# The trunk's buffers begin at multiples of 2048 bytes, and the score passes alternate between row halves

## The chip, the cores and the metric

The kernel runs on one core of a Trainium2 chip. The core has a tensor engine (TensorE, "PE" in the profile, with its weight loads shown apart as "PEld"), a vector engine (DVE), a scalar engine (ACT), a general engine (POOL) and a queue of transfers issued by SyncE (SP). They run side by side and meet only at semaphores. The metric is the device time of one execution, in microseconds; it is 1284.3 us before the change (median of 3 runs, 1284.09 to 1289.94).

## The reference

One sequence of 512 positions, width 1024, all in float32, goes through two layers:

```python
def reference(x, ...):
    # layer 0: convolution module, then gated FFN
    x = conformer_conv_module(x, ...)      # norm, 1024x2048 matmul, depthwise conv 31 taps, norm, 1024x1024 matmul
    x = conv_ffn(x, ...)                   # norm, 1024x5632 matmul, depthwise conv 3 taps, silu(gate)*up, 2816x1024
    # layer 1: differential attention, then gated FFN
    k_sh = rms_norm((rms_norm(x) @ w_k).reshape(b, s, 8, 2, 64)); v_sh = (rms_norm(x) @ w_v).reshape(b, s, 8, 128)
    q = rms_norm((rms_norm(x) @ w_q).reshape(b, s, 8, 2, 64))
    # 8 heads, 2 components c of 64 channels each, blocks of 128 query rows
    scores = einsum('bqhcd,bkhcd->bhcqk', q, k) * 64 ** -0.5
    probs = softmax(where(causal, scores, -1e30))
    diff = probs[:, :, 0] - lam * probs[:, :, 1]
    x = x + rms_norm(diff @ v) * (1 - lam_init) @ w_o
    x = conv_ffn(x, ...)
```

## The kernel before, in words

Every float32 matmul is made of three passes over rounded parts: each operand is split into a high part and the remainder (`_hi` and `_lo`, type float32r), and the passes are high x high, high x low and low x high. The activations stand channel-major: `x`, `xg_hi`, `xg_lo` (the normed input of a projection) and `act_hi`, `act_lo` (the input of the second matmul of a layer part) are 8 tiles each of 128 channels by 512 positions, 2048 bytes in each partition. A tile is the moving operand of a matmul of 512 columns at line 1034, and a 128 x 128 piece of `w_hi` or `w_lo` (512 bytes in each partition) is its stationary operand.

Weights come as one stream of 99 units of up to 128 x 2048 numbers into `w_raw`, which has two slots. ACT makes `w_hi` of a unit and DVE makes `w_lo`, one unit ahead of PE. With the input projections PE reads `xg_hi` and `xg_lo` (832 times three passes), with the output projections `act_hi` and `act_lo` (480 times three passes). For keys, queries and values the roles are swapped (line 1152): the stationary operand is a piece of `xg`, the moving one is 256 columns of a weight unit, 1024 bytes, so the starts of moving pieces alternate between two places 1024 bytes apart. In the convolution (line 1088) the stationary operand is a diagonal matrix `diag` and the moving one is `u_hi` or `u_lo` from column t on for tap t, so its start moves by 4 bytes with each tap and by 2168 bytes from tile to tile.

The attention's order is written out by hand. `attention_schedule` calls, for each of 96 pieces of the key, query and value projections, `dense` (12 matmuls of line 1152) and then the steps of `SLOTS` for the current head: turning keys and queries by transposes (`turn K`, `turn Q`), three sets of score blocks (`score A`: query block 3; `score B`: blocks 2 and 0; `score C`: block 1), softmax on ACT (line 661) with maxima on DVE (line 970), the difference of the components on DVE (`differ`, lines 979 to 982), its transposes (`turn A`, `B`, `C`, line 1171), and the product with the values (line 1214). All engines go through the same list in the same order. Block b of queries sees (b + 1) x 128 keys, so its score matmul has 512, 384, 256 or 128 columns.

Component c of a head lies in partitions 64c to 64c + 63 of `qT` and `kT`, so a score matmul uses 64 rows of the array. Its result goes to bank 4 for component 0 and to bank 5 for component 1. In `scores` PE takes one component after the other. For each block it runs the three passes and then the causal mask, a matmul of `ident16` and `mask16` in bfloat16 that uses all 128 rows and adds -1e30 above the diagonal; the mask's matmul signals `s_done`. PE waits for `e_done`, the exponentials of the set before, ahead of each set.

All of SBUF is placed by `put`, one buffer behind the other, each rounded up to 64 bytes. The build's first free byte is 16,481, so `top` is 16,512, which is 128 past a multiple of 2048. `x`, `xg_hi`, `xg_lo`, `w_raw`, `w_hi` and `w_lo` have sizes that are multiples of 2048 and all begin at 128 past a multiple of it. Behind them come parameters and constants of other sizes, and `act_hi` begins at 119,616, which is 832 past a multiple. `act_lo`, `kT`, `qT`, `v_hi` and `u_hi` also begin at 832 past a multiple.

Of the kernel before, what the change touches and what calls it, by code (L numbers as in the profile page):

```python
# [31 lines left out]
P = 128  # L32
# [9 lines left out]
HD = 64  # L42
# [59 lines left out]
SETS = [[3], [2, 0], [1]]  # L102
# [3 lines left out]
COLUMN = {3: 0, 2: 0, 0: 3 * P, 1: 0}  # L106
# [64 lines left out]
def trunk(nc, x_t, stream, params, lambdas, out_t):  # L171
    with ExitStack() as ctx:
# [4 lines left out]
            return ctx.enter_context(nc.semaphore(name))  # L177


        top = -(-nc.sbuf_base // 64) * 64  # L180

        def put(name, at, shape, dtype=F32):

            size = 2 if dtype == BF16 else 4
            end = at + -(-math.prod(shape[1:]) * size // 64) * 64
            return nc.alloc_sbuf_tensor_at(name, shape, dtype, offset=at)[(slice(None),) * len(shape)], end


        x, at = put("x", top, [P, KT, SEQ])
        xg_hi, at = put("xg_hi", at, [P, KT, SEQ], F32R)  # L190
        xg_lo, at = put("xg_lo", at, [P, KT, SEQ], F32R)
        w_raw, at = put("w_raw", at, [P, RING, SLOT])
        w_hi, at = put("w_hi", at, [P, RING, SLOT], F32R)
        w_lo, at = put("w_lo", at, [P, RING, SLOT], F32R)
        par, at = put("par", at, [P, N_PARAMS])
        ident, at = put("ident", at, [P, P])
        ones, at = put("ones", at, [P, P])
        ident16, at = put("ident16", at, [P, P], BF16)
        mask16, at = put("mask16", at, [P, P], BF16)
        small, at = put("small", at, [P, 112])  # L200

        conv_area = at
        act_hi, at = put("act_hi", at, [P, KT, SEQ], F32R)
        act_lo, area = put("act_lo", at, [P, KT, SEQ], F32R)
        eps = small[:, 0:1]
# [19 lines left out]
        sq, at = put("sq", area, [P, 2, SEQ])  # L225
        sq_sum, at = put("sq_sum", at, [P, SEQ])
        rs, at = put("rs", at, [P, SEQ])
# [3 lines left out]
        ffn_u, at = put("ffn_u", own_area, [P, 4, UP])  # L231
        ffn_t, at = put("ffn_t", at, [P, 4, SEQ])

        CP = SEQ + TAPS - 1
        conv_u, at = put("conv_u", conv_area, [P, KT, CP])
        diag, at = put("diag", at, [P, DIAGS, len(PE_TILES), 2, P], F32R)
        assert at <= area
        conv_a, at = put("conv_a", own_area, [P, 2, SEQ])
        conv_b, at = put("conv_b", at, [P, SEQ])
        conv_c, at = put("conv_c", at, [P, KT, SEQ])  # L240
        ln_sq, at = put("ln_sq", at, [P, 2, SEQ])
        u_hi, at = put("u_hi", at, [P, len(PE_TILES), CP], F32R)
        u_lo, at = put("u_lo", at, [P, len(PE_TILES), CP], F32R)
        dw_hi, at = put("dw_hi", at, [P, KT * TAPS], F32R)
        dw_lo, at = put("dw_lo", at, [P, KT * TAPS])
        lam_in, at = put("lam_in", at, [P, 4, HD])
        lam_prod, at = put("lam_prod", at, [P, 2, HD])

        v_hi, at = put("v_hi", area, [P, 2, TB, 2 * VD], F32R)
        v_lo, at = put("v_lo", at, [P, 2, TB, 2 * VD], F32R)  # L250
        k_sb, at = put("k_sb", at, [P, 2, TB, 2 * P])
        q_sb, at = put("q_sb", at, [P, 2, TB, 2 * P])
        kq_sq, at = put("kq_sq", at, [P, TB, 2 * P])
        kT_hi, at = put("kT_hi", at, [P, SEQ], F32R)
        kT_lo, at = put("kT_lo", at, [P, SEQ], F32R)
        qT_hi, at = put("qT_hi", at, [P, SEQ], F32R)
        qT_lo, at = put("qT_lo", at, [P, SEQ], F32R)
        dT_hi, at = put("dT_hi", at, [P, 10 * P], F32R)
        dT_lo, at = put("dT_lo", at, [P, 10 * P], F32R)
        prob, at = put("prob", at, [P, 2, 2, SEQ])  # L260
        o_sb, at = put("o_sb", at, [P, TB, VD])

        bank = [ctx.enter_context(nc.psum_tensor(f"bank{n}", [P, SEQ], F32)) for n in range(8)]
# [93 lines left out]
        block = ctx.enter_context(nc.Block())  # L357
# [669 lines left out]
        def _(pe):  # L1027
# [54 lines left out]
            for t in range(TAPS):  # L1082
                for n, m in enumerate(PE_TILES):
# [3 lines left out]
                    for s, (w, u) in enumerate(((0, u_hi), (0, u_lo), (1, u_hi))):  # L1087
                        got = pe.matmul(bank[CONV[n]][:, :], diag[:, t % DIAGS, n, w, :], u[:, n, t:t + SEQ],  # L1088
                                        start=(t == 0 and s == 0), stop=(t == TAPS - 1 and s == 2), skip_group_check=True)
# [84 lines left out]
            def scores(h, n):  # L1174

                if 8 * h + 2 * PLACE[SETS[n][0]]:
                    pe.wait_ge(e_done, 8 * h + 2 * PLACE[SETS[n][0]])
                for c in range(2):
                    for b in SETS[n]:
                        out = bank[4 + c][:, COLUMN[b]:COLUMN[b] + (b + 1) * P]  # L1180
                        rows = slice(c * HD, (c + 1) * HD)
                        qs = slice(b * P, (b + 1) * P)
                        for s, (q, k) in enumerate(((qT_hi, kT_hi), (qT_hi, kT_lo), (qT_lo, kT_hi))):
                            pe.matmul(out, q[rows, qs], k[rows, 0:(b + 1) * P],  # L1184
                                      start=s == 0, stop=False, skip_group_check=True)

                        pe.matmul(out[:, b * P:(b + 1) * P], ident16[:, :], mask16[:, :], start=False, stop=True,  # L1187
                                  skip_group_check=True).then_inc(s_done, 1)

            def step(h, name):  # L1190
# [16 lines left out]
                elif name == "output":  # L1207
                    pe.wait_ge(dT_l, 3 * h + 3)
                    pe.wait_ge(turned_lo, min(2 * h + 3, 2 * HEADS))
                    for b in range(TB):  # L1210
                        for k in range(b + 1):
                            at = TRI[b] + k * P
                            for n, (d, v) in enumerate(((dT_hi, v_hi), (dT_hi, v_lo), (dT_lo, v_hi))):
                                got = pe.matmul(bank[7][:, b * VD:(b + 1) * VD], d[:, at:at + P], v[:, g % 2, k, cols],  # L1214
                                                start=(k == 0 and n == 0), stop=(k == b and n == 2), skip_group_check=True)
                    got.then_inc(o_done, 1)
                elif name == "turn output":
                    pe.wait_ge(o_normed, h + 1)
                    for b in range(TB):
                        got = pe.transpose(bank[7][:, b * P:(b + 1) * P], o_sb[:, b, :], ident[:, :])  # L1220
                    got.then_inc(oT_done, 1)
                elif name == "score A":
                    pe.wait_ge(turned_lo, 2 * h + 2)
                    scores(h, 0)
                elif name.startswith("score"):
                    scores(h, LETTER[name[-1]])
                elif name == "turn A":
                    turn(h, 0)
                elif name == "turn B":
                    pe.wait_ge(dT_l, 3 * h + 1)  # L1230
                    turn(h, 1)
                elif name == "turn C":
                    pe.wait_ge(dT_l, 3 * h + 2)
                    turn(h, 2)
# [75 lines left out]
```

## Time and profile before

| what | value |
|---|---|
| median of 3 runs | 1284.3 us |
| the profiled execution's own time | 1283.49 us |
| its span, first to last instruction | 1281.7 us |
| mean granted TensorE clock | 0.991 of full |
| PE busy | 1238.3 us, 97% of the span |
| PEld busy | 1021.3 us, 80% |
| DVE busy | 843.0 us, 66% |
| ACT busy | 544.3 us, 42% |
| DMA | 81 GB/s over the span |

A busy PE in the profile is not a PE at its peak: the end of a matmul is modelled, and one matmul's shown duration laps over the next. The distance from one start to the next is what a matmul costs in a row of them. Where a stretch runs at the full granted clock, TensorE is at 2.4 GHz; at half it is at 1.2 GHz.

### The profile page before, as it was taken

The numbers are of one execution on the slowest core, as the hardware profiler recorded it, in microseconds if no ns is written. First come the engines' busy times: TensorE is split into PE (matmuls) and PEld (weight loads), VectorE is DVE, ScalarE is ACT, GpSimd is POOL, SyncE is SP. The second block draws the span as 40 slices with busy tenths as digits, with TensorE's granted clock in tenths as the row PEclk, the third lists the DMA queues.
The fourth block names the chain that finished last, engine by engine and source line by source line (L and its number), as shares of the span: only waits on it lengthen the run. The fifth ranks groups of instructions, "written<-read, shape, count | busy, mean of one in ns | idle before, by whom it ended". The sixth has DMA issues, their size and how long they took to land.

```text
span 1281.7 us, 16583 instructions
## 1 busy us (share of the span) xinstructions
PE 1238.3 (97%) x6085; PEld 1021.3 (80%) x6085; DVE 843.0 (66%) x1158; ACT 544.3 (42%) x942; POOL 111.2 (9%) x99
## 2 busy tenths in 40 slices
PE   6998997999999999999999999997999999999999
PEld 4787756788888888887998889966888888888887
DVE  7999946577627763676577777665577537762673
ACT  6256955444314431345454545433444324431441
POOL 4000001200000000002324141401200000000000
PEclk9999998999999999999999999998999999999999
DMA  5221001222322222223221212211222322232222
GB/s 212 81 91 59 1 5 53 98 76 98 109 89 98 98 99 99 81 74 109 96 70 34 67 34 67 66 33 33 99 94 91 111 69 96 98 118 79 99 74 91
DMA packets 16615, 104.00 MB, mean 81 GB/s; under 512 B 1840, under 2 KB 1968, under 8 KB 5424
## 3 DMA queue, kind: packets, MB, share of 16 engines
q1 hardware_dynamic: 16560, 103.25, 24.2%
q8 instruction: 36, 0.59, 0.2%
q14 instruction: 19, 0.16, 0.0%
HBM read 101.15 MB, written 2.10 MB: 81 GB/s over the span
## 4 chain that ended last, share of the span: by engine, by line
PE 89%; DVE 6%; ACT 3%; POOL 1%; issue 1%; DMA 0%; SPq 0%; POOLq 0%; DVEq 0%; ACTq 0%
PE bank L1034 67%; PE bank L1152 9%; PE bank L1088 5%; PE bank L1184 2%; PE bank L1214 2%; POOL sq_sum L415 1%; DVE w_lo L707 1%; DVE w_lo L699 1%; ACT prob L661 1%; DVE prob L980 1%; PE bank L1105 1%; PE bank L1187 1%; DVE prob L982 1%; PE bank L1079 1%; DMA w_raw<-stream 0%
## 5 line engine op out<-in xcount | busy, mean ns | idle before, releaser
L1034 PE MATMUL bank<-xg_hi,w_hi 128*128 128x512 f32 x832 | 326.8, 393 | 13.6 <-DVE xg_lo L715 11.1
L1034 PE MATMUL bank<-xg_lo,w_hi 128*128 128x512 f32 x832 | 325.0, 391 | 0.0
L1034 PE MATMUL bank<-xg_hi,w_lo 128*128 128x512 f32 x832 | 325.0, 391 | 0.0
L470 ACT ACTIVATE w_hi<-w_raw 128x2048 fp32r<-128x2048 f32 x83 | 158.3, 1907 | 156.5 <-PE bank L1034 156.5
L699 DVE TENSOR_TENSOR w_lo<-w_raw,w_hi 128x2048 fp32r<-128x2048 f32 x83 | 192.6, 2320 | 30.9 <-ACT w_hi L470 30.9
L1034 PE MATMUL bank<-act_hi,w_hi 128*128 128x512 f32 x480 | 193.2, 402 | 8.9 <-DVE act_lo L831 7.2
L1034 PEld LDWEIGHTS bank<-xg_hi,w_hi 128*128 128x128 f32 x832 | 156.9, 189 | 48.3 <-DVE w_lo L730 11.1
L1034 PE MATMUL bank<-act_lo,w_hi 128*128 128x512 f32 x480 | 190.8, 398 | 0.0
L1034 PE MATMUL bank<-act_hi,w_lo 128*128 128x512 f32 x480 | 190.6, 397 | 0.0
L604 ACT ACTIVATE ffn_t<-ffn_u,par 128x512 f32<-128x512 f32 x88 | 72.0, 818 | 268.6 <-DVE ffn_u L884 268.6
L1034 PEld LDWEIGHTS bank<-xg_lo,w_hi 128*128 128x128 f32 x832 | 157.0, 189 | 33.3 <-issue 0.7
L1034 PEld LDWEIGHTS bank<-xg_hi,w_lo 128*128 128x128 f32 x832 | 156.9, 189 | 32.8
L1034 PEld LDWEIGHTS bank<-act_hi,w_hi 128*128 128x128 f32 x480 | 91.1, 190 | 33.0 <-issue 8.0
L1152 PE MATMUL bank<-w_hi,xg_hi 128*128 128x256 f32 x384 | 113.7, 296 | 1.0 <-DVE xg_lo L715 1.0
L1152 PE MATMUL bank<-w_lo,xg_hi 128*128 128x256 f32 x384 | 109.1, 284 | 0.0
L1152 PE MATMUL bank<-w_hi,xg_lo 128*128 128x256 f32 x384 | 109.1, 284 | 0.0
L1034 PEld LDWEIGHTS bank<-act_hi,w_lo 128*128 128x128 f32 x480 | 90.9, 189 | 22.4
L1034 PEld LDWEIGHTS bank<-act_lo,w_hi 128*128 128x128 f32 x480 | 91.0, 190 | 21.1
L846 DVE TENSOR_TENSOR x<-bank,x 128x512 f32<-128x512 f32 x56 | 38.5, 688 | 102.2 <-PE bank L1034 102.2
L891 DVE SCALAR_TENSOR_TENSOR ffn_t<-ffn_u,par,ffn_t 128x512 f32<-128x512 f32 x88 | 65.8, 748 | 56.1 <-ACT ffn_t L604 56.1
L884 DVE TENSOR_TENSOR ffn_u<-bank,rs 128x512 f32<-128x512 f32 x88 | 60.5, 688 | 42.3 <-PE bank L1034 42.2
L1152 PEld LDWEIGHTS bank<-w_hi,xg_hi 128*128 128x128 f32 x384 | 74.3, 194 | 1.3 <-DVE xg_lo L715 1.2
(141 smaller groups left out, 1607.6 us busy)
## 6 DMA issues: line engine op xcount, KB each, us to landing
w_raw<-stream SPq DMA_DIRECT2D x87, 1024.0 KB, 4.9
w_raw<-stream SPq DMA_DIRECT2D x8, 768.0 KB, 4.3
x<-x_t SPq DMA_DIRECT2D x8, 256.0 KB, 6.8
out_t<-x SPq DMA_DIRECT2D x8, 256.0 KB, 2.0
w_raw<-stream SPq DMA_DIRECT2D x2, 512.0 KB, 5.1
par<-params SPq DMA_DIRECT2D x1, 345.5 KB, 2.9
lam_in<-lambdas SPq DMA_DIRECT2D x1, 128.0 KB, 8.6
```

Source lines behind the costliest of these rows:

```text
L415: pool.tensor_tensor(sq_sum, sq_sum, sq[:, k % 2, :], ALU.add).then_inc(sq_added, 1)
L470: act.activation(w_hi[:, j, :], w_raw[:, j, :], ACT.Copy).then_inc(w_hi_done, 1)
L604: act.activation(ffn_t[:, 2 * j + s, :], ffn_u[:, 2 * j + s, FTAPS - 1:UP], ACT.Identity, bias=p("ffn_dw_b", at + t), scale=p("ffn_dw_w", ...
L699: dve.tensor_tensor(w_lo[:, j, :], w_raw[:, j, :], w_hi[:, j, :].bitcast(F32), sub).then_inc(w_lo_done, 1)
L846: new = dve.tensor_tensor(x[:, k, :], b, x[:, k, :], ALU.add)
L884: dve.tensor_tensor(u[:, FTAPS - 1:UP], bank[2 * j + s][:, :], rs, ALU.mult).then_inc(u_done, 1)
L891: own.wait(own.mark(dve.scalar_tensor_tensor(out=v, in0=u[:, 1:1 + SEQ], scalar=p("ffn_dw_w", w + 1), in1=v, op0=ALU.mult, op1=ALU.add)))
L1034: got = pe.matmul(out, weights(w, j, k, m), v[:, k, :], start=(k == 0 and s == 0), stop=(k == count - 1 and s == 2), skip_group_check=True)
L1088: got = pe.matmul(bank[CONV[n]][:, :], diag[:, t % DIAGS, n, w, :], u[:, n, t:t + SEQ], start=(t == 0 and s == 0), stop=(t == TAPS - 1 and ...
L1152: got = pe.matmul(out, v[:, k, b * P:(b + 1) * P], w[:, j, k * 2 * P:(k + 1) * 2 * P], start=(k == 0 and s == 0), stop=(k == KT - 1 and s ...
L1184: pe.matmul(out, q[rows, qs], k[rows, 0:(b + 1) * P], start=s == 0, stop=False, skip_group_check=True)
L1214: got = pe.matmul(bank[7][:, b * VD:(b + 1) * VD], d[:, at:at + P], v[:, g % 2, k, cols], start=(k == 0 and n == 0), stop=(k == b and n == ...
```

## The change

`top` is rounded up to 2048 bytes in place of 64, and so is the start of the area that holds `act_hi` and everything behind it. The first buffer and all up to `small` move up by 1920 bytes, `act_hi` and all behind it by 3264. The bytes past a multiple of 2048 become:

| buffers | before | after |
|---|---|---|
| x, xg_hi, xg_lo, w_raw, w_hi, w_lo | 128 | 0 |
| act_hi, act_lo, kT, qT, v_hi, v_lo, dT_hi, prob, u_hi | 832 | 0 |
| diag | 1792 | 960 |
| ident | 896 | 768 |

In `scores` the loop over components becomes the innermost one, inside the loop over passes, so consecutive matmuls use rows 0 to 63 and rows 64 to 127 in turn, and write banks 4 and 5 in turn. The masks of a set come behind all its passes. The accumulation's start flag is given with the first block of a set in each bank alone.

```diff
-        top = -(-nc.sbuf_base // 64) * 64
+        HOME = 2048
+        top = -(-nc.sbuf_base // HOME) * HOME
...
-        conv_area = at
+        conv_area = -(-at // HOME) * HOME
+        at = conv_area
...
+                def block(c, b):
+                    return bank[4 + c][:, COLUMN[b]:COLUMN[b] + (b + 1) * P]
+
+                for b in SETS[n]:
+                    qs = slice(b * P, (b + 1) * P)
+                    for s, (q, k) in enumerate(((qT_hi, kT_hi), (qT_hi, kT_lo), (qT_lo, kT_hi))):
+                        for c in range(2):
+                            rows = slice(c * HD, (c + 1) * HD)
+                            pe.matmul(block(c, b), q[rows, qs], k[rows, 0:(b + 1) * P],
+                                      start=(s == 0 and b == SETS[n][0]), stop=False, skip_group_check=True)
                 for c in range(2):
                     for b in SETS[n]:
-                        out = bank[4 + c][:, COLUMN[b]:COLUMN[b] + (b + 1) * P]
-                        rows = slice(c * HD, (c + 1) * HD)
-                        qs = slice(b * P, (b + 1) * P)
-                        for s, (q, k) in enumerate(((qT_hi, kT_hi), (qT_hi, kT_lo), (qT_lo, kT_hi))):
-                            pe.matmul(out, q[rows, qs], k[rows, 0:(b + 1) * P],
-                                      start=s == 0, stop=False, skip_group_check=True)
-
-                        pe.matmul(out[:, b * P:(b + 1) * P], ident16[:, :], mask16[:, :], start=False, stop=True,
+                        pe.matmul(block(c, b)[:, b * P:(b + 1) * P], ident16[:, :], mask16[:, :], start=False, stop=True,
                                   skip_group_check=True).then_inc(s_done, 1)
```

On PE, at the first head's set A (block 3, 512 keys; bank4 belongs to component 0 and bank5 to component 1), the order before is:

```order
L1184 MATMUL bank4<-kT_hi_86,qT_hi_88 128x512
L1184 MATMUL bank4<-kT_lo_87,qT_hi_88 128x512
L1184 MATMUL bank4<-kT_hi_86,qT_lo_89 128x512
L1187 MATMUL bank4<-mask16_59,ident16_58 128x128
L1184 MATMUL bank5<-kT_hi_86,qT_hi_88 128x512
L1184 MATMUL bank5<-kT_lo_87,qT_hi_88 128x512
L1184 MATMUL bank5<-kT_hi_86,qT_lo_89 128x512
L1187 MATMUL bank5<-mask16_59,ident16_58 128x128
```

The same place on PE after the change:

```order
L1188 MATMUL bank4<-kT_hi_86,qT_hi_88 128x512
L1188 MATMUL bank5<-kT_hi_86,qT_hi_88 128x512
L1188 MATMUL bank4<-kT_lo_87,qT_hi_88 128x512
L1188 MATMUL bank5<-kT_lo_87,qT_hi_88 128x512
L1188 MATMUL bank4<-kT_hi_86,qT_lo_89 128x512
L1188 MATMUL bank5<-kT_hi_86,qT_lo_89 128x512
L1192 MATMUL bank4<-mask16_59,ident16_58 128x128
L1192 MATMUL bank5<-mask16_59,ident16_58 128x128
```

The two components now alternate, and the mask of component 0 has moved from behind three passes to behind six.

On PE in the first head's set B (blocks 2 and 0, 384 and 128 keys), from the third pass of the first block on, the order before is:

```order
L1184 MATMUL bank4<-kT_hi_86,qT_lo_89 128x384
L1187 MATMUL bank4<-mask16_59,ident16_58 128x128
L1184 MATMUL bank4<-kT_hi_86,qT_hi_88 128x128
L1184 MATMUL bank4<-kT_lo_87,qT_hi_88 128x128
L1184 MATMUL bank4<-kT_hi_86,qT_lo_89 128x128
L1187 MATMUL bank4<-mask16_59,ident16_58 128x128
L1184 MATMUL bank5<-kT_hi_86,qT_hi_88 128x384
L1184 MATMUL bank5<-kT_lo_87,qT_hi_88 128x384
L1184 MATMUL bank5<-kT_hi_86,qT_lo_89 128x384
L1187 MATMUL bank5<-mask16_59,ident16_58 128x128
```

And after the change, to the end of the set:

```order
L1188 MATMUL bank4<-kT_hi_86,qT_lo_89 128x384
L1188 MATMUL bank5<-kT_hi_86,qT_lo_89 128x384
L1188 MATMUL bank4<-kT_hi_86,qT_hi_88 128x128
L1188 MATMUL bank5<-kT_hi_86,qT_hi_88 128x128
L1188 MATMUL bank4<-kT_lo_87,qT_hi_88 128x128
L1188 MATMUL bank5<-kT_lo_87,qT_hi_88 128x128
L1188 MATMUL bank4<-kT_hi_86,qT_lo_89 128x128
L1188 MATMUL bank5<-kT_hi_86,qT_lo_89 128x128
L1192 MATMUL bank4<-mask16_59,ident16_58 128x128 x2
L1192 MATMUL bank5<-mask16_59,ident16_58 128x128 x2
```

The four masks of the set, which stood apart between groups of three passes, stand together at its end. No other instruction of any engine changes its place.

## Rows read from the trace of the kernel before

**Rows 1.** Busy times by stretch (us; x instructions; clock; DMA share; GB/s).

```profile
250.00:604.00 354.00, 353.90 (x1544) 288.79 (x1543) 219.51 (x237) 129.69 (x136) 4.64 (x5) 1.00 0.28 93
640.00:860.00 220.00, 215.02 (x1591) 192.10 (x1591) 157.86 (x337) 102.92 (x306) 58.26 (x49) 1.00 0.17 56
905.00:1281.70 376.70, 373.51 (x1628) 304.75 (x1626) 222.12 (x242) 131.18 (x133) 4.60 (x4) 1.00 0.28 94
```

**Rows 2.** PE timeline, line 1034, moving `xg`: start us, us shown, what.

```profile
300.08 0.39 PE L1034 MATMUL bank<-xg_hi,w_lo 128*128 128x512 f32 x1
...
302.12 0.39 PE L1034 MATMUL bank<-xg_hi,w_lo 128*128 128x512 f32 x1
```

**Rows 3.** PE timeline, line 1034, moving `act`.

```profile
349.70 0.39 PE L1034 MATMUL bank<-act_hi,w_hi 128*128 128x512 f32 x1
...
351.80 0.39 PE L1034 MATMUL bank<-act_hi,w_hi 128*128 128x512 f32 x1
```

**Rows 4.** PE timeline, line 1152, at half the clock, then at the full clock.

```profile
617.08 0.41 PE L1152 MATMUL bank<-w_hi,xg_hi 128*128 128x256 f32 x1
...
618.36 0.41 PE L1152 MATMUL bank<-w_hi,xg_hi 128*128 128x256 f32 x1
...
747.01 0.28 PE L1152 MATMUL bank<-w_lo,xg_hi 128*128 128x256 f32 x1
...
748.09 0.28 PE L1152 MATMUL bank<-w_lo,xg_hi 128*128 128x256 f32 x1
```

**Rows 5.** PE timeline, line 1088, the convolution.

```profile
114.82 0.63 PE L1088 MATMUL bank<-u_hi,diag 128*128 128x512 f32 x2
...
115.52 0.63 PE L1088 MATMUL bank<-u_hi,diag 128*128 128x512 f32 x2
```

**Rows 6.** PE timeline, a head's set A.

```profile
743.90 0.28 PE L1152 MATMUL bank<-w_hi,xg_lo 128*128 128x256 f32 x1
744.11 0.50 PE L1184 MATMUL bank<-kT_hi,qT_hi 64*128 64x512 f32 x1
744.45 0.39 PE L1184 MATMUL bank<-kT_lo,qT_hi 64*128 64x512 f32 x1
744.68 0.39 PE L1184 MATMUL bank<-kT_hi,qT_lo 64*128 64x512 f32 x1
745.00 0.23 PE L1187 MATMUL bank<-mask,ident 128*128 128x128 bf16 x1
745.16 0.50 PE L1184 MATMUL bank<-kT_hi,qT_hi 64*128 64x512 f32 x1
...
746.10 0.36 PE L1152 MATMUL bank<-w_hi,xg_hi 128*128 128x256 f32 x1
```

**Rows 7.** PE timeline, the same head's set B: 384 keys, then 128.

```profile
749.42 0.34 PE L1184 MATMUL bank<-kT_lo,qT_hi 64*128 64x384 f32 x1
749.60 0.33 PE L1184 MATMUL bank<-kT_hi,qT_lo 64*128 64x384 f32 x1
...
750.02 0.32 PE L1184 MATMUL bank<-kT_hi,qT_hi 64*128 64x128 f32 x1
750.18 0.27 PE L1184 MATMUL bank<-kT_lo,qT_hi 64*128 64x128 f32 x1
750.30 0.27 PE L1184 MATMUL bank<-kT_hi,qT_lo 64*128 64x128 f32 x1
750.50 0.23 PE L1187 MATMUL bank<-mask,ident 128*128 128x128 bf16 x1
```

**Rows 8.** PEld timeline, the weight load of set A's third pass.

```profile
744.45 0.18 PEld L1184 LDWEIGHTS bank<-kT_hi,qT_lo 64*128 64x128 f32 x1
```

**Rows 9.** Chain of work that ended last (start us, us, what), 684 to 709.

```profile
687.73 0.89 DVE q_sb L944 x2
...
707.68 0.63 PE bank L1205 x4
```

**Rows 10.** Waits of PE, 640 to 860: us in total, times, longest us.

```profile
PE bank L1171 <- DVE dT_lo L962: 2.6, 3, 1.0
```

## The prediction

> **What bounds the kernel now.** I read the busy times by stretch first [rows 1]. Both gated FFNs (250 to 604 and from 905 on) run at the full clock with PE busy all the time but for 3.3 us. So every nanosecond by which a matmul there gets cheaper is a nanosecond of the end. In the attention (640 to 860) PE is busy for 215.0 of 220.0 us and DVE for 157.9. PE leads there too, but not all the time, as shown below.
>
> Then I read the PE timeline for the distance between starts, because the shown durations overlap. A matmul of 512 columns with `xg` as its moving operand: 300.08 to 302.12 holds nine matmuls, 226.7 ns each [rows 2]. The same matmul with `act`: 349.70 to 351.80 holds nine, 233.3 ns each [rows 3]. What would be free of any loss comes from the clock. At half the clock (1.2 GHz) six matmuls of 256 columns take 1.28 us, 213.3 ns each, one column a cycle [rows 4]. At 2.4 GHz that makes 106.7 ns for 256 columns and 213.3 for 512. But the 256-column matmuls take 120 ns at the full clock (nine in 1.08 us [rows 4]). So each matmul loses 13.3 ns on `xg` and on moving weights, and 20 ns on `act`. The loss is there at the full clock alone, so it isn't issue; it looks like operands that are fetched too slowly.
>
> **The placement.** What is different about `act`? By the table of the change, `xg` and the weights both begin 128 bytes past a multiple of 2048, in step with each other, while `act` begins at 832, out of step with its weights. Three facts speak to which property counts.
> - Weight pieces lie 512 bytes apart and all of them cost the same, so step matters modulo 512 at most.
> - The moving pieces of line 1152 start alternately at 128 and 1152 past a multiple of 2048; only the second kind runs across a multiple of 2048. All take 120 ns [rows 4]. Running across such a multiple costs nothing by itself.
> - The convolution's moving operand begins at another place for every tap and tile, and costs about 233 ns everywhere (three matmuls in 0.70 us [rows 5]). So 233 is the ordinary price, and 226.7 the special one of operands in step.
>
> After the change `act` and the weights are both at 0, in step as `xg` and the weights are now. I take 226.7 ns for `act`: 480 x 3 = 1440 matmuls by 6.7 ns are 9.6 us. They lie where PE is always busy, but for some 66 in the attention's end, so I count all. `xg` and the weights move together and stay in step: 0. The convolution, transposes and value products move within one area: 0. The bounds are wide, because no row shows an operand that begins at a multiple of 2048. From below: all loss goes. From above: the `xg` matmuls also fall to the ordinary price.
>
> Against this stands a row: in the scores `kT` and `qT` both begin at 832, in step, and a middle pass still takes 0.23 us [rows 6]. It is one of three between switches, so I don't count it as settled.
>
> The Trainium skill ("SBUF — State Buffer", Specifications and Door 1) gives lines of 16 bytes as what reads at full bandwidth. Both 128 and 832 are multiples of 16, and by that rule the placement would change nothing. Rows 2 and 3 differ by 6.7 ns all the same, so that the trace doesn't bear it out as the whole story.
>
> **The scores: masks moved to the end.** A middle pass of 512 columns takes 0.23 us. The one before a mask takes 0.32, the mask 0.16, the first pass behind it 0.34 [rows 6]. A mask between passes thus costs 0.09 + 0.16 + 0.11 = 0.36 us, against about 0.12 for one that follows another mask. That 0.12 is not shown; it lies between 0.05 (128 columns at full clock, a quarter of the 213.3 ns) and 0.16, and I take the distance of 128-column passes [rows 7]. Saved: 0.24 us in set A, once. In set B three masks leave the middle. Before 128 columns the entry costs only 0.04 more than a middle pass (0.16 against 0.12) and the exit 0.08 (0.20 against 0.12) [rows 7]. That gives 0.09 + 0.16 + 0.04 - 0.12 = 0.17 twice and 0.08 + 0.16 + 0.11 - 0.12 = 0.23 once: 0.57. Set C has one like set A's: 0.24.
>
> **The scores: halves in turn.** A score matmul uses 64 of 128 rows. Two in a row now use different rows and different banks, so they may run side by side. Their weights still have to be loaded one after the other. The 128-column passes show what that costs: 0.12 us from start to start where the columns alone need 0.05 [rows 7]. I take 0.12 for every pass. Then the five inner distances of 0.23 in set A shrink by 0.11 each, 0.55 in all, and five of 0.18 in set B [rows 7] by 0.06 each, 0.30; set C has nothing to gain. No row shows two halves in turn. The bounds are a pair that takes as long as one pass, and a switch of halves that costs the 0.11 that a mask does.
>
> The skill ("TensorE: Matmul & The Clock Gate", The mechanism, in Part 3) says that a weight load overlaps running matmuls only where the row groups differ, and that matmuls on different row groups run at once. The first half isn't what the trace shows: the third pass's load begins at 744.45 [rows 8], as the second pass begins on the same rows, and costs nothing visible. The second half is what I count on. By "TensorEngine Tiling (Array Packing)", Key Properties, changing the mode drains the engine, which agrees with the 0.36 us of a mask in the middle.
>
> **What of it reaches the end.** The chain in the attention leaves PE at 687.73 and returns at 707.68 [rows 9]. In between it runs over softmax, differences and weight splits on DVE and ACT. That happens in every second head, and PE then waits for `dT_lo` [rows 10]. Sets B and C of that head lie inside, so that what they save turns into waiting. So of two heads, set A counts twice, B and C once. Masks: 4 x (2 x 0.24 + 0.57 + 0.24) = 5.2 us. Halves: 4 x (2 x 0.55 + 0.30) = 5.6 us. DVE now gets component 0 of a set later, with component 1. In set B it is still at its differences then, and set A's maxima are on no chain, so 0.
>
> **Sum.** The profiled execution took 1283.5 us, 1.8 more than its span; the median is 0.8 above it. 1283.5 - 9.6 - 5.2 - 5.6 = 1263.1, and 1263.9 on the median's scale. I say 1264.
>
> **Rivals.**
> - *Pairs also load their weights together.* A pair then costs one pass: 0.03 less in set A, 0.18 + 0.36 in set B, 0.36 in set C, or 4 x 0.96 = 3.8 us more: 1260.1. Nothing in the trace speaks for it.
> - *The halves don't run side by side.* The 5.6 stay out: 1269.5. The three passes of one half show nothing about it.
> - *The placement changes nothing*, the 6.7 ns having another cause, such as how high in memory `act` lies: 1273.5. The scores' middle pass speaks for it.
> - *Switching halves costs what a mask does.* 0.10 each over five inner distances in sets A and C and about 0.8 in all in B outweigh the masks: 4 x (2 x 0.26 + 0.25 + 0.26) = 4.1 us lost: 1283.5 - 9.6 + 4.1, so 1278.8.
> - *A start at a multiple of 2048 frees the fetch altogether.* 2496 x 13.3 ns = 33.3 us, 1440 x 20 = 28.8, 1152 x 13.3 = 15.3 of which two thirds count, and the scores' 10.8: 1201. Line 1152's two starts speak against it, but neither of them is a 0.
> - *Slower: `xg` falls out of its good step.* If 226.7 belongs to a start at 128 rather than to being in step, `xg` and line 1152 go to the ordinary price: 2496 x 6.7 = 16.6 and 1152 x 6.7 = 7.7 us more, and `act` gains nothing: 1283.5 + 24.3 - 10.8, so 1297.8. It decides from 10.8 us over 3648 matmuls, 3.0 ns each, on. The scores' middle pass (in step at 832, not fast) speaks for it, and the change of `xg`'s own start is what could set it off.
>
> **How the numbers follow.** Forecast 33%, loads together 12%, no side by side 18%, placement without effect 14%, costly switches 4%, all loss gone 6%, slower 9%, neither part doing anything 4%. A measurement here tells 0.5% (6.4 us) from no change. Faster than 1277.9: 33 + 12 + 18 + 14 + 6 = 83%. Within: 4 + 4 = 8%. Slower: 9%. The range from 1254 to 1279 holds the first four and the costly switches, 81%.
>
> **What would show it.** Nine `act` matmuls in 2.04 us; `xg` still at 226.7; 256 columns still at 120. In set A the six passes start about 0.12 us apart, or 0.23 if the halves don't overlap, and set A goes from 1.99 us (744.11 to 746.10) to about 1.2. PE waits more than 2.6 us for `dT_lo`. I am wrong if `xg` changes its distance either way, or if `act` keeps 233.

## The result and the profile after

| | before | after |
|---|---|---|
| median | 1287.1 us (4 runs, 1284.1 to 1291.6) | 1270.25 us (4 runs, 1269.6 to 1270.6) |
| profiled execution, span | 1283.5, 1281.7 us | 1270.6, 1268.7 us |
| its mean granted clock | 0.991 | 0.982 |

The ratio is 0.9865 [0.9829, 0.9902]: the change makes the kernel faster by 1.35%. On the scale of the 1284.3 us given before, that is 1267 us; the forecast was 1264.

First the busy times of the changed kernel in the same stretches as [rows 1] (PE, PEld, DVE, ACT, POOL, each in us and instructions; granted clock; DMA share; GB/s). The last row is a stretch at the attention's end.

```profile
250.00:604.00 354.00, 353.74 (x1557) 291.51 (x1556) 221.50 (x240) 131.93 (x143) 7.08 (x6) 1.00 0.29 95
640.00:860.00 220.00, 201.43 (x1616) 185.00 (x1614) 166.00 (x359) 104.98 (x321) 56.43 (x47) 0.98 0.17 54
905.00:1268.70 363.70, 360.60 (x1587) 297.33 (x1586) 217.67 (x237) 126.90 (x128) 1.73 (x2) 1.00 0.29 94
863.00:875.00 12.00, 8.86 (x37) 7.64 (x36) 1.13 (x5) 1.83 (x9) 1.20 (x2) 0.50 0.00 1
```

The FFNs are as full as before and simply do more matmuls per microsecond (1557 against 1544 in 354 us). The attention has changed its character: PE is busy for 201.4 of 220 us where it was 215.0, and DVE has gone from 157.9 to 166.0.

Now the placement, on the PE timeline (start us, us shown, what): a row of matmuls moving `xg`, then one moving `act`, to be compared with [rows 2, 3].

```profile
300.03 0.39 PE L1036 MATMUL bank<-xg_hi,w_hi 128*128 128x512 f32 x1
...
302.07 0.39 PE L1036 MATMUL bank<-xg_hi,w_hi 128*128 128x512 f32 x1
...
348.99 0.39 PE L1036 MATMUL bank<-act_hi,w_hi 128*128 128x512 f32 x1
...
351.03 0.39 PE L1036 MATMUL bank<-act_hi,w_hi 128*128 128x512 f32 x1
```

Nine distances take 2.04 us on both: `act` now costs 226.7 ns as `xg` does, `xg` has kept its price, and the 256-column matmuls of the projections are still at 120 ns.

The same head's set A, which answers to [rows 6] ("x2" puts two matmuls of one kind together; in the trace they start 3 to 4 ns apart):

```profile
735.53 0.50 PE L1188 MATMUL bank<-kT_hi,qT_hi 64*128 64x512 f32 x2
735.87 0.40 PE L1188 MATMUL bank<-kT_lo,qT_hi 64*128 64x512 f32 x2
736.11 0.39 PE L1188 MATMUL bank<-kT_hi,qT_lo 64*128 64x512 f32 x2
736.43 0.29 PE L1192 MATMUL bank<-mask,ident 128*128 128x128 bf16 x2
736.52 0.36 PE L1154 MATMUL bank<-w_hi,xg_hi 128*128 128x256 f32 x1
```

Set A takes 0.99 us (735.53 to 736.52) where it took 1.99. Two passes now cost what one did, weight loads and all, and a second mask starts 0.07 us behind the first, where the forecast had 0.12. Set B goes from 2.91 to 1.21 us and set C from 1.29 to 0.65. Over the 24 sets, from the first score matmul to the next other one, PE spends 22.9 us where it spent 49.6. The saving on PE is thus 26.7 us.

Only part of that reaches the end. The waits of PE in 640 to 860 say where the rest is (us in total, times, longest):

```profile
PE bank L1173 <- DVE dT_lo L964: 11.1, 10, 3.1
PE bank L1188 <- ACT prob L663: 2.4, 3, 0.8
PE bank L1210 <- DVE dT_lo L964: 1.7, 2, 1.4
PE bank L1173 <- DVE prob L984: 0.9, 1, 0.9
```

[Rows 10] had 2.6 us in 3 waits. The chain of work that ended last shows why. DVE's share of it went from 6 to 10% and PE's from 89 to 84%. Besides the part of [rows 9], which is still there, there is now a second DVE part in the heads between, which ends at the same instruction:

```profile
708.27 0.89 PE bank L1188 x6
...
709.36 1.29 DVE small L972 x2
...
721.24 0.61 DVE dT_lo L964
...
721.90 0.66 PE bank L1173 x4
```

So in every head, and no longer in every second one, the end runs through the softmax, the differences and the weight splits on DVE.

The granted clock is the other thing to see in the profile after. From 862.4 on TensorE was granted half its clock (1.2 GHz) for 17.1 us, as the row 863 to 875 above shows. What it did before that, in busy times again, first of the changed kernel, then of the kernel before:

```profile
828.00:862.00 34.00, 26.27 (x172) 19.80 (x169) 22.38 (x54) 13.56 (x48) 1.21 (x2) 1.00 0.10 32
```

```profile
828.00:862.00 34.00, 32.46 (x187) 24.37 (x185) 19.71 (x45) 14.82 (x47) 2.41 (x4) 1.00 0.19 63
```

PE idles for 7.7 of these 34 us, where it was 1.5. But the two rows don't lie equally close to a fall of the clock. The profile before has only 6.8 us at half the clock in the attention's end, from 882.5 on, and in the 34 us ahead of that PE idled for 6.0:

```profile
848.50:882.50 34.00, 28.04 (x165) 21.23 (x163) 16.09 (x41) 11.79 (x46) 2.40 (x4) 1.00 0.01 1
```

So 7.7 us of idling were followed by 17.1 us at half the clock and 6.0 by 6.8; what makes the difference isn't shown. Over the whole span it is 46.6 us after and 25.8 before.

### The profile page after: what moved, and what is told of

Same layout as the page of the kernel before. It is cut to its first block, busy times and chain, and to the rows that moved or that the text cites. A ratio compares the mean times of both kernels' runs of the same rounds, so it can differ in the third digit from the quotient of the medians.

```text
span 1268.7 us, 16583 instructions
## 1 busy us (share of the span) xinstructions
PE 1213.7 (96%) x6085; PEld 1014.2 (80%) x6085; DVE 843.9 (67%) x1158; ACT 542.1 (43%) x942; POOL 111.8 (9%) x99
## 4 chain that ended last, share of the span: by engine, by line
PE 84%; DVE 10%; ACT 3%; POOL 1%; issue 1%; DMA 0%; SPq 0%; POOLq 0%; DVEq 0%; ACTq 0%
PE bank L1036 67%; PE bank L1154 7%; PE bank L1090 5%; PE bank L1219 2%; DVE prob L982 1%; DVE w_lo L709 1%; DVE small L972 1%; ACT prob L663 1%; DVE w_lo L701 1%; DVE prob L984 1%; POOL sq_sum L417 1%; DVE dT_lo L964 1%; PE bank L1107 1%; ACT w_hi L472 1%; PE bank L1188 1%
## 5 line engine op out<-in xcount | busy, mean ns | idle before, releaser
L1036 PE MATMUL bank<-xg_hi,w_hi 128*128 128x512 f32 x832 | 327.1, 393 | 13.3 <-DVE xg_lo L717 10.9
L1036 PEld LDWEIGHTS bank<-xg_hi,w_hi 128*128 128x128 f32 x832 | 156.9, 189 | 48.2 <-DVE w_lo L732 10.8
```

The source lines that it names most:

```text
L1036: got = pe.matmul(out, weights(w, j, k, m), v[:, k, :], start=(k == 0 and s == 0), stop=(k == count - 1 and s == 2), skip_group_check=True)
```

## The experiments

All ratios are to the kernel before on the same chip. Its own time moves with the mean clock that it was granted: 1283.2 us (median of 19 runs) at 0.991 and 0.992, 1286.6 (20 runs) at 0.984 and 0.985, 1290.4 (10 runs) at 0.980 to 0.983. I compare runs at equal clock where medians would mix them. Such a comparison is rough: a level holds times up to 4 us apart (1285.3 to 1289.4 at 0.984 and 0.985), and it leaves out whatever the change itself does to the clock.

**place.** The placement alone.

```diff
-        top = -(-nc.sbuf_base // 64) * 64
+        HOME = 2048
+        top = -(-nc.sbuf_base // HOME) * HOME
...
-        conv_area = at
+        conv_area = -(-at // HOME) * HOME
+        at = conv_area
```

> The two starts are rounded up to 2048, the scores stay as before. Theory (operands in step): act matmuls go from 233.3 to 226.7 ns, xg stays; 1440 x 6.7 = 9.6 us, ratio to before about 0.9925, and no change in the attention but for its 66 act matmuls. Rival (the placement needs the scores' change, or helps nothing by itself): act stays at 233.3, ratio 1.000.

Measured: 1281.2 us (10 runs), ratio 0.9963 [0.9943, 0.9983]; `act` at 226.7 ns. That looks like half of the expected gain, but all ten runs were granted 0.981 to 0.985. At 0.984 and 0.985 it took 1278.6 (3 runs) against 1286.6, and at 0.980 to 0.983 1281.6 (7 runs) against 1290.4: the placement brings 8.0 to 8.8 us at equal clock. In the profile the part up to the attention is 4.1 us shorter, but the attention itself is longer, with 50.9 us at half the clock in the span.

**scores.** The other half alone: the hunk of `scores` on the old placement, `act` at 233.3 ns.

> The halves alternate and the masks come last; the placement stays as before. Theory (the attention is now bound by DVE's chain): the score sections on PE go from 49.6 to about 23 us, but only 3 to 6 us of it reach the end, ratio 0.995 to 0.998; PE waits for dT_lo over 12 us, and TensorE's clock is at half for longer. Rival (the two parts are independent and each gives what the forecast said): ratio 0.9916.

Measured: 1277.95 us (5 runs), 0.9949 [0.9927, 0.997]; at 0.984 and 0.985 1277.4 (4 runs) against 1286.6, that is 9.1 less, and 10.6 less in the one run at 0.982 (1279.8 against 1290.4). By the ratio it is a little more than the 3 to 6 us expected. PE waits for `dT_lo` in 640 to 860 are 10.7 + 2.5 us in 12 waits, and the sets take 22.95 us of PE. At equal clock the parts add up. At 0.984 and 0.985 they are 8.0 + 9.1 = 17.1, and the full change takes 1270.2 (2 runs), 16.4 less. At 0.980 to 0.983 they are 8.8 + 10.6 = 19.4, and the full change takes 1270.25 (6 runs), 20.1 less. They are two separate gains.

**masks_last.** Masks behind the passes, components one after the other, old placement.

```diff
                 for c in range(2):
                     for b in SETS[n]:
...
+                            pe.matmul(block(c, b), q[rows, qs], k[rows, 0:(b + 1) * P],
+                                      start=(s == 0 and b == SETS[n][0]), stop=False, skip_group_check=True)
+                for c in range(2):
+                    for b in SETS[n]:
+                        pe.matmul(block(c, b)[:, b * P:(b + 1) * P], ident16[:, :], mask16[:, :], start=False, stop=True,
```

> Old placement, one component after the other as before, but the masks of a set behind all its passes. The forecast's step: set A 0.24 us shorter, set B 0.57, set C 0.24, so set A 1.75, B 2.35, C 1.05 us; with masks in a row at 62 ns as in the changed kernel, some 0.06 less each. Of 8.8 us in all 3 to 5 reach the end by the forecast; if DVE's chain takes it, under 2, ratio above 0.998.

Measured: 1279.3 us (8 runs), 0.9949 [0.9927, 0.997]. The timeline of its first set A:

```profile
654.26 0.50 PE L1186 MATMUL bank<-kT_hi,qT_hi 64*128 64x512 f32 x2
654.60 0.40 PE L1186 MATMUL bank<-kT_lo,qT_hi 64*128 64x512 f32 x2
654.83 0.40 PE L1186 MATMUL bank<-kT_hi,qT_lo 64*128 64x512 f32 x2
655.16 0.28 PE L1190 MATMUL bank<-mask,ident 128*128 128x128 bf16 x2
655.26 0.36 PE L1152 MATMUL bank<-w_hi,xg_hi 128*128 128x256 f32 x1
```

Component 1's three passes stand behind all three of component 0 in the program, and yet by the records they start with them, in pairs 6 to 10 ns apart (the profile doesn't name the half, but each half has just one pass of each pair of operands in this set). The halves run side by side without being in turn. I had expected 1.75 us for set A; it takes 1.00. What kept the halves apart before was the mask between the components; no run separates whether that is because it uses all 128 rows or because it is of another type. In set B, where one half has six passes in a row, the second half starts only when the first block of the first half is through:

```profile
658.30 0.44 PE L1186 MATMUL bank<-kT_hi,qT_hi 64*128 64x384 f32 x1
...
658.76 0.44 PE L1186 MATMUL bank<-kT_hi,qT_hi 64*128 64x384 f32 x2
...
659.98 0.36 PE L1152 MATMUL bank<-w_hi,xg_hi 128*128 128x256 f32 x1
```

There the overlap is partial, and set B takes 1.68 us against 1.21 in turn. Of the 26.7 us of PE time this version has 22.9 (49.6 to 26.7); being in turn adds 3.8 more, nearly all in set B, and at 0.984 and 0.985 nothing that can be told from zero (1277.9 in 5 runs against 1277.4 in 4).

The Trainium skill ("TensorE: Matmul & The Clock Gate", The mechanism) has weight loads for other row groups pulled ahead of running matmuls, and tiles on different row groups starting some 4 ns apart; the pairs agree with both (3 to 4 ns in the changed kernel). It also says that matmuls keep the program's order in start and end. The starts recorded here don't: the second half's first pass starts at 654.27, ahead of the first half's second at 654.60.

**step128.** The old start of the first buffer; the activations' area 128 past a multiple of 2048, in step with the weights but not at a multiple.

```diff
-        conv_area = at
+        conv_area = -(-at // 2048) * 2048 + 128
+        at = conv_area
```

> The base stays at 128 past a multiple of 2048, the act area begins at 128 past one too; the scores stay as before. Theory (being in step with the weights counts): 226.7 ns for act, as with the start at 0, ratio 0.9925. Rival (a start at a multiple of 2048 counts): act stays at 233.3, ratio 1.000.

Measured: 1277.8 us (6 runs), 0.9944 [0.9923, 0.9965]. The line is that of the `act` matmuls again:

```profile
348.85 0.39 PE L1035 MATMUL bank<-act_hi,w_hi 128*128 128x512 f32 x1
...
350.89 0.39 PE L1035 MATMUL bank<-act_hi,w_hi 128*128 128x512 f32 x1
```

Nine in 2.04: 226.7 ns. The whole gain of the placement is had without a start at a multiple of 2048 (at 0.984 and 0.985 1277.8 in 4 runs, where place had 1278.6). It is the start of one operand against the other that counts.

**step384 and step256.** As step128, but 256 and 128 bytes out of step with the weights (`+ 128 + 256`, `+ 128 + 128`).

> As step128 but the act area begins at 384 past a multiple of 2048, 256 bytes out of step with the weights at 128; scores as before. Theory A (the pattern repeats within 256 bytes): 226.7 ns for act. Theory B (it repeats only with 512, the distance of the weight pieces): about 233 ns for act.

> As step128 but the act area begins at 256 past a multiple of 2048, 128 bytes out of step with the weights at 128; scores as before. Theory A (the pattern repeats with 128 bytes): 226.7 ns for act. Theory B (with 256): about 233 ns or a value between.

Measured for step384: 1276.75 us (6 runs), 0.9924 [0.9898, 0.9951]; for step256: 1288.2 (10 runs), 1.0014 [0.9997, 1.0031]. First step384, then step256, in the same row of matmuls:

```profile
348.70 0.39 PE L1035 MATMUL bank<-act_hi,w_hi 128*128 128x512 f32 x1
...
350.74 0.39 PE L1035 MATMUL bank<-act_hi,w_hi 128*128 128x512 f32 x1
```

```profile
349.22 0.39 PE L1035 MATMUL bank<-act_lo,w_hi 128*128 128x512 f32 x1
...
351.32 0.40 PE L1035 MATMUL bank<-act_lo,w_hi 128*128 128x512 f32 x1
```

256 bytes out of step cost 226.7 ns, 128 bytes 233.3. So 256 bytes are as good as none, as they would be if the pattern repeats after 256 bytes; the kernel before was 704 out of step (832 - 128), which is 192 beyond a multiple of 256. How high in memory `act` lies isn't the cause, which the prediction had as a rival: step256 lies between step128 and step384, 128 bytes from each, and it alone keeps 233.3.

**xg_off.** The full change with `xg` moved on by 64 bytes.

```diff
+        at += 64
         xg_hi, at = put("xg_hi", at, [P, KT, SEQ], F32R)
         xg_lo, at = put("xg_lo", at, [P, KT, SEQ], F32R)
+        at = -(-at // HOME) * HOME
```

> The changed kernel with xg_hi and xg_lo 64 bytes further on, at 64 past a multiple of 2048, and the weights back at a multiple. Theory (a moving operand 64 bytes out of step with its stationary one pays 6.7 ns more): the 2496 matmuls on xg go from 226.7 to 233.3 ns, 16.6 us more than the changed kernel, ratio to before about 1.000; act stays at 226.7. Rival (act's area alone is special, or low addresses are): xg stays at 226.7, time as the changed kernel.

Measured: 1272.0 us (4 runs), 0.9895 [0.9862, 0.9927], with `xg` at 228.9 ns:

```profile
299.35 0.39 PE L1038 MATMUL bank<-xg_hi,w_lo 128*128 128x512 f32 x1
...
301.41 0.39 PE L1038 MATMUL bank<-xg_hi,w_lo 128*128 128x512 f32 x1
...
629.99 0.28 PE L1156 MATMUL bank<-w_hi,xg_hi 128*128 128x256 f32 x1
...
631.05 0.28 PE L1156 MATMUL bank<-w_hi,xg_hi 128*128 128x256 f32 x1
```

I had expected the ordinary price on both kinds, and that missed. 64 bytes out of step cost 2.2 ns a matmul, a third of what 128 do. With the roles swapped, where the weights move and `xg` stands still, the same 64 bytes make it faster: nine in 1.06 us, 117.8 ns instead of 120. "In step is best" thus holds for the 512-column matmuls that were tried, not for every shape.

**light_before and light_after.** Both kernels with one DVE instruction per block less; it shortens DVE's chain and touches PE in nothing. They leave out the scaling of the second component's probabilities, so their output isn't the reference's.

```diff
-                    own.wait(own.mark(dve.tensor_scalar(prob[:, n % 2, 1, w], prob[:, n % 2, 1, w],
-                                                        inv[:, 2 * b + 1:2 * b + 2], neg_lam, ALU.mult, ALU.mult)))
```

> The kernel before, with one DVE operation per score block left out: the second component's probabilities are not scaled by the reciprocal sum and lambda (32 operations, about 20 us of DVE's 158 in the attention). Theory (DVE's chain holds PE only in every second head here): a gain of at most the 5 us that PE waited, ratio about 0.997. Rival (DVE never mattered): 1.000.

> The changed kernel with the same operation left out. Theory (the 26.7 us that PE saves in the score sections are taken by DVE's chain): with DVE lighter, 8 us or more of them come through, so it is at least 20 us faster than the lighter kernel before, and over 8 us faster than the changed kernel; PE's waits for dT_lo fall from 14 to under 6 us. Rival (the saving is lost to something else, the clock or PE itself): it gains no more over the changed kernel than 5 us.

Measured: 1282.7 us (10 runs), 0.9972 [0.9948, 0.9995] on the kernel before, and 1255.3 (4 runs), 0.9754 [0.9717, 0.9792] on the changed one. The same cut is worth 3 us before and 15 after. Between the two stand 27.4 us; light_before had 0.988 as its median clock, and against its four runs at 0.991 and 0.992 (1278.9) it is 23.6. Without the placement's 8 to 9, 15 to 19 us are left of the scores' 26.7, where the full kernel has 9 to 11. Part of that is the clock. In the profile of light_after TensorE is at half the clock for 24.9 us, in that of the changed kernel for 46.6, and all four runs had 0.989 or 0.990. The waits for `dT_lo` fall too. This is light_after in 640 to 880, which holds the attention's end in both; the changed kernel has 14.4 us in 11 waits there, the longest 3.2:

```profile
PE bank L1171 <- DVE dT_lo L964: 7.5, 4, 2.4
```

That is more than the under 6 expected, so DVE's chain isn't all gone.

**late_b.** The full change with `turn B` moved to the next head's first slot, so that PE meets it later.

```diff
-SLOTS = [["turn K"], [], ["turn C"], ["turn Q"], ["output"], ["score A"], ["norm output"], ["score B"],
-         [], ["turn A", "turn output"], ["score C"], ["turn B"]]
-LATE = ("turn C", "output", "norm output", "turn output")
+SLOTS = [["turn K", "turn B"], [], ["turn C"], ["turn Q"], ["output"], ["score A"], ["norm output"], ["score B"],
+         [], ["turn A", "turn output"], ["score C"], []]
+LATE = ("turn B", "turn C", "output", "norm output", "turn output")
```

> The changed kernel with the step turn B moved from the head's last slot to the first slot of the next head, on all engines. Theory: PE's waits of 3.3 us at turn B (in every second head) and 0.7 to 0.9 (in the others) shrink because DVE has 1.4 us more time, 4 to 8 us in all; ratio to before 0.981. Rival (the work is only moved, turn C or turn Q wait instead): as the changed kernel, 0.9865, or 1 to 3 us slower than it.

Measured: 1278.9 us (9 runs), 0.9933 [0.9913, 0.9954], slower than the changed kernel by 7 to 9 us (the ratios 0.9865 and 0.9876 of its two sets of runs against 0.9933), which is more than the rival had, too. The first row is late_b's in 640 to 880, the second that of the changed kernel:

```profile
PE bank L1173 <- DVE dT_lo L964: 20.8, 9, 5.2
```

```profile
PE bank L1173 <- DVE dT_lo L964: 14.4, 11, 3.2
```

The idea failed. Waits are fewer but longer: DVE goes through the same list, so its own work on set B moves back with the step. A chain that binds isn't shortened by meeting its end later. TensorE is at half the clock for 56 us, 10 more than in the changed kernel, which is part of the loss.

**fold.** The full change with less on DVE's chain: the two quotients per block are replaced by one ratio. The norm behind it forgets a common factor, if its epsilon is scaled by sum0 squared.

```diff
-                    own.wait(own.mark(dve.reciprocal(inv[:, 2 * b:2 * b + 2], prob_sum[:, 2 * b:2 * b + 2])))
-                    own.wait(own.mark(dve.tensor_scalar(prob[:, n % 2, 1, w], prob[:, n % 2, 1, w],
...
+                    inverse = own.mark(dve.reciprocal(ratio[:, b:b + 1], sum1))
+                    own.mark(dve.scalar_tensor_tensor(out=eps_row[:, b:b + 1], in0=sum0, scalar=EPS, in1=sum0,
+                                                      op0=ALU.mult, op1=ALU.mult))
...
+                    dve.scalar_tensor_tensor(out=prob[:, n % 2, 0, w], in0=prob[:, n % 2, 1, w],
+                                             scalar=ratio[:, b:b + 1], in1=prob[:, n % 2, 0, w],
```

> The changed kernel, with the softmax's first reciprocal left to the norm behind it: DVE forms p0 + p1 x (lambda x sum0 / sum1) in one large operation per block, and the norm's epsilon is multiplied by sum0 squared per row. DVE loses 32 large operations (20.4 us) and gains 64 of one column (about 0.15 us each, 9.6 us). Theory (DVE's chain holds the attention): faster than the changed kernel by 4 to 10 us, ratio to before 0.979 to 0.983. Rival (small operations in a chain of waits cost as much as the large one): as the changed kernel.

**after_again** is the changed kernel on the same chip.

> The changed kernel once more, on the chip of the other three, to compare with: ratio to before 0.9865 within its interval.

Measured: fold 1265.4 us (4 runs, 1264.3 to 1266.8), 0.9844 [0.9819, 0.9868]; after_again 1270.2 (4 runs, 1269.5 to 1271.6), 0.9876 [0.9853, 0.9898]. No run of the one reaches the other; the 4.8 us between them are at the low end of what was expected, and the ratio misses its range. fold is the fastest of the versions that compute everything. In its profile the projections of keys, queries and values with the heads among them (first to last matmul of that line) take 205.5 us, 210.1 and 208.9 in the two profiles of the changed kernel and 201.6 in light_after: the shorter DVE's part, the shorter the heads.

## Why the prediction was right, and where its steps were not

- **Placement, 9.6 us by 1440 x 6.7 ns: right.** The distance fell by just that. In the two profiles the part up to the attention is 3.9 us shorter and the second FFN 3.4, and the 192 output projections of the attention add up to 1.3 by the same distance, 8.6 together; at equal clock 8.0 to 8.8. The reason given, operands in step, is what step128 shows. The bound that a start at a multiple of 2048 frees all the loss is out, and so is the slower rival: `xg` kept 226.7. The row that the prediction held against itself stays unexplained: a middle pass of the scores, whose `kT` and `qT` are in step before and after, still takes 0.23 to 0.24 us.
- **Masks and halves: the size on PE was off.** The forecast had raw savings of 8.4 and 6.8 us, 15.2 together; PE got 26.7. Two terms failed. The halves' weight loads were to go one after the other at 0.12 us; they go together, as the rival "pairs also load their weights together" had it. And a mask behind another was put at 0.12; it is 0.06 to 0.07. The split was wrong in kind as well: moving the masks was itself what let the halves overlap, 22.9 us, and the turn-taking on which I had put nearly half adds 3.8 (masks_last).
- **What reaches the end: 10.8 forecast, 9.1 to 10.6 measured at equal clock.** Here the step "in every second head sets B and C turn into waiting" was too kind. It put 4.4 of 15.2 us into waiting and let 71% through; of the 26.7 us about a third comes through (34 to 40%). The two profiles say where the rest went, from the first projection of keys, queries and values to the attention's last matmul (before, then after):

```profile
610.50:914.30 303.80, 290.08 (x2024) 256.44 (x2023) 204.37 (x416) 137.21 (x378) 79.29 (x65) 0.98 0.18 59
606.60:904.80 298.20, 272.43 (x2024) 248.46 (x2024) 205.19 (x416) 134.89 (x378) 79.23 (x65) 0.95 0.18 59
```

  The stretch is only 5.6 us shorter. PE's idle time in it rises from 13.7 to 25.8 us, so 12.1 us went into waiting, 9.4 of them for `dT_lo` (6.9 to 16.3), since DVE's chain took over in the other heads too. The time at half the clock rises from 10.2 to 30.7 us. As a 256-column matmul takes 213.3 ns there and 120 otherwise, I estimate the 20.5 us more at a loss of 9.0. The forecast had no term for that. A saving larger than forecast met a bound nearer than forecast, and the errors nearly cancelled. The forecast came out well partly by that luck.
- **"Set A's maxima are on no chain": no longer so.** In the heads between, the chain after the change goes from set A's masks straight to the maxima (`DVE small L972` at 709.36). For set A the 0 put for it still holds: component 0's mask starts 0.90 us into set A, where it was 0.89.
- **The sum.** 1283.5 was a run at a clock of 0.991, and the changed kernel was granted 0.982 to 0.984 in all eight of its runs. How the 7 us between 1263.1 and 1270.2 divide can't be said closely. From the kernel before at 0.984 and 0.985, 1286.6, the change takes 16.4 us off (2 runs), 4 less than the forecast's 20.4, and the other 3 are the clock of the run that the sum began with. From the kernel before at 0.980 to 0.983, 1290.4, it takes 20.1 off (6 runs), and nearly all 7 are the clock.
- **What would show it:** `act` in 2.04 us, `xg` and 256 columns unchanged, more than 2.6 us of waits for `dT_lo`: all seen. Set A at 1.2 us was 0.99.

Open is why the changed kernel is never granted 0.991. How much PE idles ahead of the fall doesn't settle it. Place idles for 3.7 of 34 us and then has 17.1 us at half the clock; light_after idles for 7.3 of 34 and then has 6.8 (these two rows):

```profile
838.50:872.50 34.00, 30.26 (x169) 22.52 (x170) 21.86 (x54) 13.69 (x47) 1.20 (x2) 1.00 0.10 32
823.00:857.00 34.00, 26.74 (x177) 21.01 (x175) 16.15 (x43) 12.38 (x48) 2.41 (x4) 1.00 0.01 4
```

Place was never granted more than 0.985 either, in ten runs. Open too is what makes the distance depend on 256 bytes, and what the remaining 13.3 ns are.

## What to carry to other kernels

Read the distance between starts for each pair of operands, not the mean duration. Where the same matmul costs differently from two buffers, compare the two operands' starts with each other before changing anything else. One full-array matmul between two half-array groups (here also of another type) can cost the overlap of the whole groups; gather such matmuls at the end and look in the timeline whether the halves then run together by themselves. And before spending effort on PE in a stretch where another engine is nearly as busy, take one instruction out of that engine in both versions: the difference shows how much of a saving can come through, if the clock is read beside it.

## What the hardware showed unexpectedly

- A 128 x 128 by 512 matmul in float32r at the full clock costs, by the moving operand's start less the stationary one's modulo 256: 226.7 ns at 0 (three placements), 228.9 at 64, 233.3 at 128 and at 192. With 256 columns of weights moving it is 120 ns at 0 and about 118 at -64, so the sign, the shape or the kind of operand matters.
- Score matmuls on the two row halves overlap in full, weight loads as well, whether they are issued in turn or three and three; issued six and six (set B) they overlap in part. Two cost what one costs (0.23 to 0.24 us for 512 columns).
- Masks in bfloat16 in a row start 0.06 to 0.07 us apart.
- The time at half the clock differed from run to run of one and the same kernel, with mean clocks near 0.991, 0.985 and 0.981 and times of 1283, 1287 and 1290 us (the kernel before). A comparison of 0.5% needs that column beside the times.
